# The NSA compression and its compressed branch are woven between the eight feature tiles of z's projection

## The reference, cut to what matters

```python
q, kc, vc, ks, vs, kw, vw, gate, z = jnp.split(u @ w_in, points, axis=-1)
k_cmp = compress(kc, pe_k, w1_k, w2_k)      # silu((blocks + pe) @ w1) @ w2
v_cmp = compress(vc, pe_v, w1_v, w2_v)      # 31 overlapping blocks of 32 tokens, 4 groups
...
s_c = einsum('bqgjd,bcgd->bgjqc', qblk, k_cmp) + bias_c      # 16 heads x 31 blocks
p_c = softmax(where(m_c, s_c, NEG)) * any(m_c)
o_c = einsum('bgjqc,bcgd->bqgjd', p_c, v_cmp)                # the compressed branch
...
o = gate[0] * o_c + gate[1] * o_s + gate[2] * o_w            # o_s, o_w: 512 keys each
return (o * silu(z)) @ w_out
```

## Time and profile before

| | us |
|---|---|
| median of 3 runs | 2366.68 (2364.24 to 2367.32) |
| the profiled execution | 2365.17 |
| its span, first to last instruction | 2363.4 |
| TensorE busy in the span | 2103.8 (89%) |
| ScalarE, GpSimd, VectorE busy | 934.2, 901.9, 841.6 |
| TensorE's share of the chain that ended last | 72% |

### The profile page before, as it was taken

The page is one execution under the profiler, slowest core; times in us unless marked ns, Lnnn a source line. Parts: engine busy times, 40 slices in busy tenths (PEclk is TensorE's granted clock), DMA queues, the critical chain, the costliest instruction groups (busy, mean ns, idle before and its releaser), DMA issues.

```text
span 2363.4 us, 33687 instructions
## 1 busy us (share of the span) xinstructions
PE 2103.8 (89%) x13673; PEld 1698.8 (72%) x13674; DVE 841.6 (36%) x1794; ACT 934.2 (40%) x1701; POOL 901.9 (38%) x631
## 2 busy tenths in 40 slices
PE   4999889989989869996589589998997898999898
PEld 3898756678766746775577478886877667888687
DVE  2100357430027365147453643343023254334301
ACT  3332157552237354442123244443134445444312
POOL 2422057534447322241003524544433552444442
PEclk9998589999999879798588799999999899999999
DMA  4322100123320211221111223333222212333322
GB/s 121 92 66 67 32 28 2 36 59 106 89 81 1 67 45 51 73 65 28 41 31 32 80 65 96 99 98 107 98 72 72 72 37 66 95 98 98 98 98 80
DMA packets 222649, 162.10 MB, mean 69 GB/s; under 512 B 30663, under 2 KB 205327, under 8 KB 222496
## 3 DMA queue, kind: packets, MB, share of 16 engines
q1 hardware_dynamic: 220016, 151.83, 21.7%
q0 software_dynamic: 2480, 8.12, 1.2%
HBM read 154.69 MB, written 5.24 MB: 68 GB/s over the span
## 4 chain that ended last, share of the span: by engine, by line
PE 72%; DVE 9%; ACT 4%; issue 3%; POOL 1%; POOLq 1%; DMA 0%; DVEq 0%; SPq 0%; ACTq 0%; PEld 0%; PEldq 0%
PE ps L361 13%; PE ps L331 11%; PE ps L335 11%; PE ps L332 10%; PE ps L371 6%; PE ps L1272 2%; PE ps L1283 2%; PE ps L1296 2%; PE ps L2714 1%; PE ps L1045 1%; PE ps L1613 1%; PE ps L2000 1%; PE ps L2010 1%; ACT buffer L622 1%; PE ps L1633 1%
## 5 line engine op out<-in xcount | busy, mean ns | idle before, releaser
L273 POOL TENSOR_TENSOR weights_lo<-buffer,weights_hi 128x1024 fp32r<-128x1024 f32 (+1 forms) x265 | 653.9, 2469 | 1048.1 <-ACT weights_hi L262 1047.8
L262 ACT ACTIVATE weights_hi<-buffer 128x1024 fp32r<-128x1024 f32 (+1 forms) x265 | 276.3, 1045 | 337.6 <-PE ps L371 302.4
L331 PE MATMUL ps<-u_hi,weights_hi 128*128 128x512 f32 (+1 forms) x752 | 282.2, 379 | 7.2 <-DVE u_lo L649 6.8
L332 PE MATMUL ps<-u_lo,weights_hi 128*128 128x512 f32 (+1 forms) x752 | 281.5, 378 | 0.0
L1821 ACT ACTIVATE buffer<-ps,buffer 128x512 f32<-128x512 f32 x88 | 68.5, 779 | 278.3 <-PE ps L335 278.3
L335 PE MATMUL ps<-u_hi,weights_lo 128*128 128x512 f32 (+1 forms) x752 | 176.7, 378 | 0.0
L1851 DVE SCALAR_TENSOR_TENSOR buffer<-ps,buffer,buffer 128x511 f32<-128x511 f32 x88 | 66.0, 750 | 287.7 <-ACT buffer L1821 287.7
L331 PEld LDWEIGHTS ps<-u_hi,weights_hi 128*128 128x128 f32 x752 | 143.6, 191 | 33.5 <-DVE u_lo L649 7.3
L332 PEld LDWEIGHTS ps<-u_lo,weights_hi 128*128 128x128 f32 x752 | 143.8, 191 | 25.5
L335 PEld LDWEIGHTS ps<-u_hi,weights_lo 128*128 128x128 f32 x752 | 136.7, 191 | 25.8
L877 DVE RECIPROCAL buffer<-buffer 128x1 f32<-128x1 f32 x24 | 3.8, 159 | 345.6 <-ACT buffer L805 345.5
(11 more groups left out here) (391 smaller groups left out, 4333.9 us busy)
## 6 DMA issues: line engine op xcount, KB each, us to landing
buffer<-in_w_up SPq DMA_DIRECT2D x88, 512.0 KB, 3.8
buffer<-in_w_down SPq DMA_DIRECT2D x44, 512.0 KB, 3.4
buffer<-in_diff_w_in SPq DMA_DIRECT2D x32, 512.0 KB, 4.0
buffer<-in_nsa_w_in SPq DMA_DIRECT2D x28, 512.0 KB, 3.8
buffer<-in_w_rkv SPq DMA_DIRECT2D x24, 512.0 KB, 4.1
buffer<-in_nsa_w_out SPq DMA_DIRECT2D x8, 512.0 KB, 3.6
buffer<-in_diff_w_out SPq DMA_DIRECT2D x8, 512.0 KB, 3.6
buffer<-in_norm_g POOLq DMA_DIRECT2D x8, 512.0 KB, 4.4
```

What stands on the lines that cost most here:

```text
L262: self.nc.scalar.activation(self.part_hi[:, part % self.PARTS, 0:n], self.raw[:, ld % self.RAW, 0:n], ACT.Copy).then_inc(self.hi_ready, 1)
L273: self.nc.gpsimd.tensor_tensor(self.part_lo[:, part % self.PARTS, 0:n], self.raw[:, ld % self.RAW, 0:n], self.part_hi[:, part % self.PARTS ...
L331: nc.tensor.matmul(out, hi[:, k, :], rhs[0][:, k, tokens], start=(k == 0), stop=False)
L332: nc.tensor.matmul(out, hi[:, k, :], rhs[1][:, k, tokens], start=False, stop=False)
```

## The change

The stage `NsaCompress` is gone, `NsaProject` ends with the gates, and `NsaCompressed` holds z's eight tiles, the compression and the compressed branch. z's tiles use banks 0 and 1. The w1 blocks stand between z's blocks in the ring. `warm_up` is taken out. The branch's working buffers move from the place of `nsa_u_lo`, which z's tiles still read, into columns 0 to 255 of the bias; so the wide copy of these columns is done at the end of the stage, strips 0 to 5 by VectorE and 6 to 15 by GpSimd, and each strip is one head. All four engines but TensorE wait for each other at the stage's end; TensorE waits for the last take of z and of the branch's output.

```diff
-    def warm_up(self):
-        for _ in range(WARM_UP):
-            self.nc.tensor.matmul(self.ps[:, 7, :], self.hot[:, 0:P], self.hot[:, 0:512], start=True, stop=True)
...
-        dve.wait_ge(self.bias_taken, 8)
-        step(nc.vector.tensor_copy(self.bias[:, :, 0:2 * P],
-                                   self.bias[:, :, 2 * P:2 * P + 1].to_broadcast([P, HEADS, 2 * P])))
+    def repeat(self, copy, first, end):
+        return copy(self.bias[:, first:end, 0:2 * P], self.bias[:, first:end, 2 * P:2 * P + 1].to_broadcast([P, end - first, 2 * P]))
...
+        z = lambda: load_features(env, w, NSA_IN - D + P * len(self.z), P)[0]
+        self.z.append(z())
         for name in ("nsa_cmp_w1_k", "nsa_cmp_w1_v"):
...
+                self.w1.append(env.load(w1[:, k:k + 8, :], split=False))
...
+            self.z.append(z())
+        while len(self.z) < KD:
+            self.z.append(z())
...
+    def wait_taken(self, pe):
+        pe.wait_ge(self.env.proj_taken, self.z[-1][1] + 1)
+        pe.wait_ge(self.o_taken, NT)
...
+        tr.then_inc(self.pe_rows_turned, 1)
+        project(0)
+        pe.wait_ge(env.proj_taken, g_gates + NT)
+        pe.wait_ge(self.pe_cols, 1)
+        hidden(0)
+        project(1)
+        hidden(1)
+        project(2)
+        pe.wait_ge(self.hid_taken, 2)
...
+        bias(0)
+        project(3)
+        pe.wait_ge(self.keys_ready, 1)
         scores(0)
         for i in range(NT):
             if i + 1 < NT:
+                bias(i + 1)
                 scores(i + 1)
+            project(i + 4)
             pe.wait_ge(self.p_scaled, i + 1)
...
+    def gpsimd(self, pool, step):
+        nc, m = self.env.nc, self.m
+        self.env.split_lo(pool, self.z[-1][0])
+        pool.wait_ge(self.pT_ready, NT)
+        pool.wait_ge(self.s_ready, NT)
+        self.setup.repeat(nc.gpsimd.tensor_copy, m.STRIPS_LATE, HEADS)
...
+        split(1)
+        take(0)
+        split(2)
+        act.wait_ge(self.hid_bias_taken, 1)
+        act.wait_ge(self.hid_ready, 1)
...
         exp(0)
         for i in range(NT):
             if i + 1 < NT:
                 exp(i + 1)
+            take(i + 4)
+            split(i + 6)
             act.wait_ge(self.o_ready, i + 1)
...
+        dve.wait_ge(self.o_ready, NT)
+        step(self.setup.repeat(nc.vector.tensor_copy, 0, m.STRIPS_LATE))
...
-        env.warm_up()
+        self.compressed.wait_taken(pe)
...
+    STRIPS_LATE = 6
...
+        strips = bias[:, :, 0:2 * P]
+        self.vbd, self.pcT = strips[:, 0:4, :], strips[:, 4:6, :]
+        self.pc = strips[:, 6:8, :]
+        self.sc = strips[:, 8:12, :].rearrange("p (b s) c -> p b s c", b=2)
+        self.kcmp = strips[:, 12, 0:GROUPS * NCP].rearrange("p (g c) -> p g c", c=NCP)
+        self.hid = strips[:, 13, :]
```

More of the change, by code:

```diff
@@ L94 @@
 N_VEC = V_CONV + 2 * 176
-WARM_UP = 16
 class Env:
@@ L939, in tensor @@
         project_tokens(env, pe, [ld], u, g)
-        for ld, g in self.z:
-            project_features(env, pe, ld, u, g)
     def vector(self, dve, step):
@@ L954, in gpsimd @@
                            io[name][0].rearrange("(k two) d -> k (two d)", two=2)).then_inc(m.small_arrived, 16)
-        self.env.split_lo(pool, self.z[-1][0])
+        self.env.split_lo(pool, self.gates[0] + 1)
     def scalar(self, act, step):
@@ L1050, in tensor @@
             mm.then_inc(self.hid_ready, 1)
-        pe.wait_ge(self.hid_taken, 2)
-        nc.tensor.matmul(env.ps[:, 4, 0:GROUPS * NC], m.w2[:, 0:128], m.hid[:, 0, 0:GROUPS * NC], start=True, stop=True)
-        for g in range(GROUPS):
-            mm = nc.tensor.matmul(env.ps[0:NC, 5, g * DH:(g + 1) * DH], m.hid[:, 1, g * NC:(g + 1) * NC],
-                                  m.w2[:, 128:192], start=True, stop=True)
-        mm.then_inc(self.cmp_ready, 1)
-    def scalar(self, act, step):
-        env, nc, m = self.env, self.env.nc, self.m
-        act.wait_ge(self.hid_bias_taken, 1)
-        for kv in range(2):
-            act.wait_ge(self.hid_ready, kv + 1)
-            nc.scalar.activation(m.hid[:, kv, 0:GROUPS * NC], env.ps[:, 6 + kv, 0:GROUPS * NC], ACT.Silu,
-                                 bias=m.hid_bias[:, 2 * kv:2 * kv + 1]).then_inc(self.hid_taken, 1)
@@ L1081, with bias @@
[L1081 to L1096 removed]
+        def bias(i):
@@ L1103, in scores @@
             mm.then_inc(self.bias_ready, 1)
+        def scores(i):
             if i:
@@ L1112, in scores @@
             mm.then_inc(self.s_ready, 1)
+        _, g_gates = self.gates
+        pe.wait_ge(env.proj_taken, g_gates)
+        pe.wait_ge(m.small_arrived, 16 * 5)
+        for kv in range(2):
+            tr = nc.tensor.transpose(env.ps[:, 1, kv * CMP_K:(kv + 1) * CMP_K], m.pe_rows[0:CMP_K, kv, :],
+                                     env.ident[0:CMP_K, 0:CMP_K])
+        tr.then_inc(self.pe_rows_turned, 1)
[7 more added lines that the diff above has]
+        pe.wait_ge(self.hid_taken, 2)
+        nc.tensor.matmul(env.ps[:, 4, 0:GROUPS * NC], m.w2[:, 0:128], m.hid[:, 0:GROUPS * NC], start=True, stop=True)
+        for g in range(GROUPS):
+            mm = nc.tensor.matmul(env.ps[0:NC, 5, g * DH:(g + 1) * DH], m.hid[:, P + g * NC:P + (g + 1) * NC],
+                                  m.w2[:, 128:192], start=True, stop=True)
+        mm.then_inc(self.cmp_ready, 1)
+        bias(0)
+        project(3)
+        pe.wait_ge(self.keys_ready, 1)
         scores(0)
@@ L1140, in exp @@
                 act.wait_ge(self.pT_ready, i)
-            nc.scalar.activation(m.pc, m.sc[:, i % 2, :], ACT.Exp).then_inc(self.p_ready, 1)
+            nc.scalar.activation(m.pc, m.sc[:, i % 2, :, :], ACT.Exp).then_inc(self.p_ready, 1)
+        split(1)
[3 more added lines that the diff above has]
+        act.wait_ge(self.hid_ready, 1)
+        nc.scalar.activation(m.hid[:, 0:GROUPS * NC], env.ps[:, 6, 0:GROUPS * NC], ACT.Silu,
+                             bias=m.hid_bias[:, 0:1]).then_inc(self.hid_taken, 1)
+        take(1)
+        split(3)
+        act.wait_ge(self.hid_bias_taken, 2)
+        act.wait_ge(self.hid_ready, 2)
+        nc.scalar.activation(m.hid[:, P:P + GROUPS * NC], env.ps[:, 7, 0:GROUPS * NC], ACT.Silu,
+                             bias=m.hid_bias[:, 2:3]).then_inc(self.hid_taken, 1)
+        take(2)
+        split(4)
+        take(3)
+        split(5)
         exp(0)
@@ L1165, in take @@
             for odd in range(2):
-                part = m.sc[:, i % 2, :].rearrange("p (h two c) -> p h two c", two=2, c=NCP)[:, :, odd, :]
-                add = nc.vector.tensor_tensor(part, env.ps[:, 7 - 5 * odd, 0:256].rearrange("p (h c) -> p h c", c=NCP),
+                part = m.sc[:, i % 2, :, :].rearrange("p s (h two c) -> p s h two c", two=2, c=NCP)[:, :, :, odd, :]
+                add = nc.vector.tensor_tensor(part, env.ps[:, 7 - 5 * odd, 0:256].rearrange("p (s h c) -> p s h c", s=2, c=NCP),
                                               part, ALU.add)
@@ L1241, with __init__ @@
 class NsaAttend(PairAttend):
-    def __init__(self, env, m, ahead):
+    def __init__(self, env, m, ahead, compressed):
         super().__init__(env, "nsa_", [(k, i, br) for k in range(KD) for i in (3, 1, 2, 0) for br in range(2)], 8)
-        self.m, self.ahead = m, ahead
+        self.m, self.ahead, self.compressed = m, ahead, compressed
         self.o_gated = env.sem("nsa_o_gated")
@@ L3037, in build @@
             Norm(env, pre[0], m.u, setup.x_arrived),
-            NsaProject(env, m, setup),
-            NsaCompress(env, m),
-            NsaCompressed(env, m),
-        ]
-        nsa = NsaAttend(env, m, len(env.loads) + 2)
+        ]
+        project = NsaProject(env, m, setup)
+        compressed = NsaCompressed(env, m, setup, project)
+        nsa = NsaAttend(env, m, len(env.loads) + 2, compressed)
+        stages += [project, compressed]
         stages += [
```

133 lines of the change are left out of this document (64 added, 69 removed).

## The result

The changed kernel takes 2336.1 us in the median of four executions (2328.6 to 2342.1), the kernel before 2365.5 beside it: a ratio of 0.988, 95% interval 0.985 to 0.990. Forecast were 2325.7 us and a range of 2312 to 2341. The range holds the time, the sign is right, and the number is 10.4 us too low; the price of rival B, 2336, is met. The profiled execution is the fastest of the four (2328.6 us, span 2326.7).

What follows compares the result with a forecast made beforehand. It took TensorE's half clock and waits in the compression and compressed branch as the bound. Stage terms of 85.7 against 130.15 us saved 44.5, less 3.5 for clock falls: 41.0 off 2365.17, plus 1.51 to the median, 2325.7; range 2312 to 2341.

Steps and rivals of the forecast that it cites:

- rival B: Compression groups still halve the clock, each some 4 us full then half, next tile slow: 10 us, 2336; chance 0.2.
- At 2.4 GHz it is half, 0.43: Compression: a step of 0.85 us at 1.2 GHz takes 0.43 at full clock, 13.8 us in the sum.
- The clock behind scores 1: Compressed branch: narrow matmuls halve the clock, costing 2.5 us in scores 1 and z's fifth tile, 1.0 for other pairs.
- z's first tile: Start of the stage: z's tiles still begin at 1.2 GHz behind the gates, 1.9 us more than dense tiles.
- VectorE's copy ahead of the values: Compressed branch: between transposes and values, TensorE waits 0.8 us for this copy.
- seven table loads: ScalarE in the stage: loads of 1.28 us fit its turns; by the skill's sum, at most 0.6 us more in total.
- GpSimd's strips: End of the stage: ten strips of the bias copy take 3.8 us, hidden; the other bound adds 2.0.
- Rival D: ScalarE's queue or a late block holds TensorE in each turn, 3 us a turn, 2338 in all; chance 0.08.
- The warm-up, priced at nothing: Start of the attention: removing 5.13 us of matmuls gains 0, bounds +5 and -3, as TensorE waits for GpSimd.
- same 8.3 us: Start of the attention: the time said to stay, with TensorE waiting for GpSimd after the barrier.
- The gain's source: Compressed branch: z tiles cover waits for VectorE and ScalarE; without this cover each turn would wait 3.6 us.

Runs made afterwards that it cites:

- e12: The changed kernel run once more, unaltered: median 2338.0 us of six executions.
- e5: The changed kernel with ScalarE writing keys and values apart by even and odd token, so compression steps read neighbouring columns, result the same: 2325.4 us.
- e7: The kernel before with keys and values written apart and read as neighbouring columns, nothing else: 2362.5 us, ratio 0.9997.
- e1: The changed kernel with each compression step's second matmul reading 31 neighbouring columns per group, hence other data: 2325.1 us.
- e10: The kernel of e5 with z's tile 1 moved ahead, so both compression groups follow each other: 2325.9 us.
- e2: The changed kernel with compression steps put two at a time between the matmul pairs of z's second and third tile: 2340.9 us.
- e9: The kernel of e2 with z's second and third block loaded ahead of the second half of each compression weight: 2327.3 us.
- e4: The changed kernel with the three splits of the output projection's weights moved behind units 13, 21 and 29 of the attention: 2328.5 us.
- e3: The changed kernel with the sixteen warm-up matmuls put back ahead of the attention's first scores: 2336.6 us.
- e8: The changed kernel's single stage unwoven: all z tiles first, then both compression groups, then the compressed branch alone: 2357.5 us.

## Why the prediction was right in sign and range, and 10 us off

Against the profile of before, the changed one gained 28.7 us in the stage, 0 in the attention and 9.2 in the rest, and lost 1.1 ahead of the stage: 36.8. The rest is put down to chance (e12), so the change is worth about 28 us. That is what the medians say (2336.1 against 2365.5), and 41.0 were forecast.

**The step that failed: "At 2.4 GHz it is half, 0.43".** A full-clock step took 0.63. Rows taken at 1.2 GHz were scaled by the clock, but at 2.4 GHz a pass over columns 16 apart takes longer than half. e5 and e7 show it from both sides: neighbouring columns bring 0.44 at the full clock and nothing at half. With 32 steps this is (0.63 - 0.43) x 32 = 6.4 us of the sum. The Trainium skill had a rule for it that the prediction did not draw on: "SBUF — State Buffer", in the note on "cachelines" of its section "Door 1: The DMA port swizzle", says that each access that crosses to a new line of 16 bytes pays, and gives 4 as the distance that is free for fp32. Columns 16 apart are beyond that, and the traces agree in direction at 2.4 GHz (0.47 against 0.30 us a pair) but show no cost at 1.2 GHz.

**The fall inside the groups** was rival B, given 0.2. It came, and it came with the reading at a distance: over neighbouring columns, with steps of 0.44, it is absent (e1, e5), even over 14.4 us (e10). B had the price from 4 us at the full clock; measured were 6.6 (187.5 to 194.1) and 6.0 (205.2 to 211.2). Both groups together took 22.2 us where 13.8 stood in the sum, 8.4 more; of this 6.4 are the longer steps and 2.0 the half clock. The tiles behind them lost 1.25 and 2.45 us. So the fall of the clock cost 5.7 us where B charged 10, and the longer steps, which B did not have, 6.4. That the total met B's 2336 is luck. One argument against B, that nothing is left idle inside the groups, was no protection: TensorE was busy throughout. Here the rule of the Trainium skill, "TensorE: Matmul & The Clock Gate", section "HAM oscillation — how this bites in real kernels", by which idle gaps bring the clock down, fits e2, where the clock fell in a stop of 4.75 us; it does not explain the changed kernel's groups, which have no gap.

**The clock behind scores 1** fell in the place named. Scores 1 took 3.22 us and not 1.8, tile 4 7.4 and not 5.45, 3.4 together where 2.5 were charged; the other two pairs, charged 1.0, lost nothing. So this term of 3.5 holds for this profile. Its size is not fixed: scores 1 and tile 4, 10.7 us here, took 9.1 in the same kernel's second profile (e12) and 7.5 in e9, where no fall came. The groups' 8.4, the 3.7 of the two tiles behind them and some 0.4 in what is left of the stage are the 12.5 us between 89.2 and 101.7.

**Right:** z's first tile (7.3 us, 5.45 + 1.9 forecast); VectorE's copy ahead of the values 0.78; no z tile waited for its weights, although ScalarE waited 24.1 us for two blocks, as forecast without reaching TensorE; seven table loads (5.1 + 3.8 us on ScalarE) that hold up nothing; VectorE's strips 0.96. GpSimd's strips were over-sized (3.8, measured 2.32), at no cost either way. Rival D had its place but not in this kernel: a late block did hold TensorE in e2, as soon as the steps stood where the load order did not foresee them.

**The warm-up, priced at nothing:** right within the spread. The transposes start 9.1 us behind the barrier as forecast, set by GpSimd's splits (e4). (The prediction's "same 8.3 us" are not in its rows, where the transposes stand 8.6 us behind the first split, 310.81 to 319.44; no term hangs on it. After the change they are 7.8, 283.16 to 290.96.) The 1.9 us for their slow start that the prediction named and then left at 0 are there, 2.3 us by e3; but against the kernel before, whose attention took the same 146.2 us, the 0 stands.

**The gain's source** was named rightly: e8 shows that the weaving, not the missing barriers, carries three quarters of it.

## What to carry to other kernels

A duration taken at half the clock gives the full-clock one only if everything in it follows the clock: look for operands read at a distance, and take the row of a pass over neighbouring columns beside it. When narrow steps are woven between dense tiles, look at how they read as well as how many they are: laying the operand out so that they read neighbouring columns was worth 13 us of the stage here, twice the 6 us that the shorter step explains (the other 7 are falls of the clock that were absent or shorter), and nothing where the clock was already low. Re-ordering steps on one engine re-orders what the load queue must bring; go through the ring of slots again, and compare profiles part by part, since parts that nobody touched vary by 12 us.

## What the runs showed of the hardware

- The pair of passes over 124 columns 16 apart takes 0.47 us at 2.4 GHz (187.65 to 188.12) and 0.57 at 1.2 (196.38 to 196.95), that over neighbouring columns 0.30 (188.49 to 188.79, in e5) and 0.56 (236.13 to 236.69, in e7).
- The clock is not a matter of TensorE being busy: 11.00 us busy in 11.00 went down to a mean of 0.80; 14.40 busy in 14.40, with the same matmuls but neighbouring columns, stayed at 1.00; 23.90 in 23.90 of these very steps, begun at 0.50, stayed at 0.50.
- In the stages that were not changed, the same work takes from 1892.3 to 1904.5 us over fourteen profiles. One stretch of it took 443.0 us at a mean clock of 0.83 and 452.9 at 0.81: the clock's falls differ from profile to profile.
